# Eight raw weight places with in-place low parts, four places for high parts, and experts without a loop, in a two-block transformer on one core

## The reference

```python
def first_block(x, c, ...):
    cs = jax.nn.silu(c)
    for l in range(2):
        mod = cs @ w_ada[l] + b_ada[l]
        h = rmsnorm(x, g_pre[l]) * (1 + scale) + shift
        y = hybrid_mixer(h, w_in[l], w_out[l], ...)
        x = x + gate * rmsnorm(y, g_post[l])
    return x
```

## Time and profile before

| | |
|---|---|
| median of three runs | 1647.71 us |
| the profiled execution | 1648.49 us, its span 1646.7 us |
| mean granted TensorE clock | 0.94 of full speed |
| PE, DVE, ACT busy | 1420.0, 1216.3, 861.3 us |
| bytes of DMA | 403.08 MB, mean 245 GB/s |
| stages (us of the span) | pre to 47, lay0 to 255, lay1 to 465, na to 632, ffn to 884, mla to 1000, go to 1020, experts to 1553, `more` to 1619 |

### The profile page before, as it was taken

The page is one execution under the profiler, slowest core; times in us unless marked ns, Lnnn a source line. Parts: engine busy times, 40 slices in busy tenths (PEclk is TensorE's granted clock), DMA queues, the critical chain, the costliest instruction groups (busy, mean ns, idle before and its releaser), DMA issues.

```text
span 1646.7 us, 21231 instructions
## 1 busy us (share of the span) xinstructions
PE 1420.0 (86%) x7628; PEld 1189.7 (72%) x7628; DVE 1216.3 (74%) x1484; ACT 861.3 (52%) x1210; POOL 65.5 (4%) x82
## 2 busy tenths in 40 slices
PE   2798996989869986899985896999999999999992
PEld 1687776877658865898974785877777777777772
DVE  8676657766566646788866535889889888899885
ACT  0443544435443543344323544577677777777772
POOL 0000000000010000000001004000000000000001
PEclk9989998999988997999997996999999999999996
DMA  9763524735246632677773214799999999999782
GB/s 400 296 258 110 198 103 162 283 118 193 102 155 254 238 120 97 258 309 282 267 270 122 103 52 145 272 342 364 353 343 366 341 351 366 336 368 353 289 366 89
DMA packets 61538, 403.08 MB, mean 245 GB/s; under 512 B 6535, under 2 KB 9735, under 8 KB 15117
## 3 DMA queue, kind: packets, MB, share of 16 engines
q1 hardware_dynamic: 52416, 379.45, 60.7%
q10 hardware_dynamic: 7020, 15.17, 2.6%
q0 software_dynamic: 2016, 7.34, 1.2%
HBM read 393.01 MB, written 8.91 MB: 244 GB/s over the span
## 4 chain that ended last, share of the span: by engine, by line
PE 49%; DVE 31%; ACT 9%; issue 7%; DMA 2%; POOL 1%; ACTq 0%; DVEq 0%; SPq 0%; POOLq 0%
DVE w_lo L2175 18%; PE PS L826 13%; PE PS L828 12%; PE PS L827 12%; ACT w_hi L1601 4%; DVE acc L2192 3%; ACT xg L1695 2%; PE PS L978 1%; PE PS L998 1%; DMA raw<-in_ws 1%; DVE a_lo L2335 1%; PE PS L896 1%; DVE hb L2346 1%; DVE hb L2344 1%; DVE h_lo L2301 1%
## 5 line engine op out<-in xcount | busy, mean ns | idle before, releaser
L2175 DVE TENSOR_TENSOR w_lo<-raw,w_hi 128x2048 fp32r<-128x2048 f32 x287 | 659.5, 2298 | 147.7 <-ACT w_hi L1601 124.8
L1601 ACT ACTIVATE w_hi<-raw 128x2048 fp32r<-128x2048 f32 x287 | 547.7, 1918 | 235.1 <-PE PS L828 222.9
L826 PE MATMUL PS<-w_hi,h_hi 128*128 128x512 f32 (+2 forms) x812 | 336.6, 415 | 24.7 <-DVE h_lo L2596 7.3
L827 PE MATMUL PS<-w_lo,h_hi 128*128 128x512 f32 (+2 forms) x812 | 319.4, 393 | 0.0
L828 PE MATMUL PS<-w_hi,h_lo 128*128 128x512 f32 (+2 forms) x812 | 319.2, 393 | 0.0
L826 PE MATMUL PS<-h_hi,w_hi 128*128 128x256 f32 x776 | 235.4, 303 | 24.1 <-DVE h_lo L2220 11.2
L828 PE MATMUL PS<-h_hi,w_lo 128*128 128x256 f32 x776 | 227.1, 293 | 0.0
L827 PE MATMUL PS<-h_lo,w_hi 128*128 128x256 f32 x776 | 227.1, 293 | 0.0
L826 PEld LDWEIGHTS PS<-w_hi,h_hi 128*128 128x128 f32 x812 | 156.3, 192 | 72.0 <-DVE w_lo L2175 15.1
L2192 DVE SCALAR_TENSOR_TENSOR acc<-raw,cs,acc 128x512 f32<-128x512 f32 x252 | 189.5, 752 | 8.9
L828 PEld LDWEIGHTS PS<-w_hi,h_lo 128*128 128x128 f32 x812 | 156.1, 192 | 32.7
(11 more groups left out here) (310 smaller groups left out, 1405.8 us busy)
## 6 DMA issues: line engine op xcount, KB each, us to landing
raw<-in_ws SPq DMA_DIRECT2D x359, 1024.0 KB, 5.7
y_rows<-ysb ACTq DMA_DIRECT2D x10, 512.0 KB, 7.0
rp<-in_rp ACTq DMA_DIRECT2D x8, 384.0 KB, 4.7
ckb<-in_ck ACTq DMA_DIRECT2D x2, 1024.0 KB, 4.8
y_rows<-ones ACTq DMA_DIRECT2D x3, 512.0 KB, 9.2
x<-in_x SPq DMA_DIRECT2D x1, 1024.0 KB, 11.3
gpost<-in_gpost ACTq DMA_DIRECT2D x2, 512.0 KB, 5.3
x_rows<-xn_f ACTq DMA_DIRECT2D x2, 512.0 KB, 3.8
```

What stands on the lines that cost most here:

```text
L826: t.matmul(out, lhs[0], rhs[0], start=start, stop=False, skip_group_check=True)
L827: t.matmul(out, lhs[0], rhs[1], start=False, stop=False, skip_group_check=True)
L1601: a.activation(wh[:, SPL_AT[e.phase][i], :], raw[:, r, :], ACT.Copy).then_inc(*e.inc("hi"))
L2175: v.tensor_tensor(wl[:, s, :], raw[:, r, :], wh[:, s, :].bitcast(F32), ALU.subtract).then_inc(*e.inc("raw_used"))
```

## The change

1. RAW = 8 and SPL = 4. The low part is written over the raw step: `w_lo` is a second name for the memory of `raw`, so that there are 8 + 4 = 12 places of the same size. A place of a "w" step is now free when PE has done the block (`split_used`); that of an "ada" step still at `raw_used`. `ring_plan` gets, for each step, the semaphore that releases it.
2. The experts are moe0 to moe7, all written out on PE, ACT, DVE and SP. `more` is still a loop. `expert()` itself is not edited on any engine; its calls move with SPL.
3. The list of steps of lay has its last four "ada" halves after w12 to w15, where they were after w11 to w14; that of na has halves after w2 to w5 and w7 to w14, where it had them after w2 to w13.
4. Calls of `hi_to` and `split_to` in lay, na, mla move by one block, and by ticks in mla. In ffn, DVE's `split_to(n + 2 + SPL)` becomes `split_to(n + 1 + SPL)`, the same block as before, and ACT's `hi_to(n + 2 + SPL)` is one block further.

The core of the diff:

```diff
-RAW = 6
-SPL = 3
+RAW = 8
+SPL = 4
...
 def layer_steps():
-    halves = dict(zip((2, 3, 4, 5, 7, 8, 9, 10, 11, 12, 13, 14), ...))
+    halves = dict(zip((2, 3, 4, 5, 7, 8, 9, 10, 12, 13, 14, 15), ...))
...
 def na_steps():
-    halves = dict(zip(range(2, 14), ...))
+    halves = dict(zip((2, 3, 4, 5, 7, 8, 9, 10, 11, 12, 13, 14), ...))
...
+def raw_released(p, i):
+    if STEPS[p][i][0] == "w":
+        return "split_used", STEPS[p][i][1]
+    return "raw_used", i
+RAW_AT, RAW_NEED = ring_plan(RAW, {p: len(STEPS[p]) for p in PHASES}, raw_released)
+SPL_AT, SPL_NEED = ring_plan(SPL, SPLITS, lambda p, i: ("split_used", i))
...
-        wl = sb("w_lo", [P, SPL, STEP], F32R)
+        wl = nc.alloc_sbuf_tensor_at("w_lo", [P, RAW, STEP], F32R, offset=at[0] - 4 * RAW * STEP - 4 * SPL * STEP)
```

SP, `stream`:

```diff
-                        sp.wait_ge(*e.at("raw_used", RAW_NEED[phase][i]))
+                        sp.wait_ge(*e.at(*RAW_NEED[phase][i]))
```

DVE, `raw_to`:

```diff
-                        v.tensor_tensor(wl[:, s, :], raw[:, r, :], wh[:, s, :].bitcast(F32),
+                        v.tensor_tensor(wl[:, r, :], raw[:, r, :], wh[:, s, :].bitcast(F32),
```

PE (ACT, DVE and SP alike):

```diff
-                with pe.Fori(0, LOOPS) as rep:
-                    for p in TWO:
-                        e.enter(p, rep)
-                        expert()
-                e.enter("moeZ")
-                expert()
+                for p in EXPERTS[1:]:
+                    e.enter(p)
+                    expert()
```

ACT, lay:

```diff
-                hi_to(5)
+                hi_to(6)
                 slot(0)
-                hi_to(7)
+                hi_to(8)
                 slot(1)
                 ada_out(0, 1)
-                hi_to(8)
+                hi_to(9)
                 slot(2)
...
-                hi_to(9)
+                hi_to(10)
                 ada_out(1, 1)
```

In na, ACT's hi_to 5, 7, 9 become 6, 8, 10; in mla, its 5, 7, 8, 9 become 6, 8, 9 and none. DVE, ffn:

```diff
-                    split_to(n + 2 + SPL)
+                    split_to(n + 1 + SPL)
```

DVE, lay:

```diff
-                split_to(5)
+                split_to(6)
...
-                split_to(9)
+                split_to(10)
                 dve.wait_ge(*e.at("g_tanh", 1))
...
                 logits(0)
```

DVE, na, in the ticks:

```diff
-                    split_to(min(na_steps_before(i) + SPL, 15) if i < 14 else 16)
+                    split_to(min(na_steps_before(i) + SPL, 16))
```

More of the change, by code:

```diff
@@ L31 @@
 T_CMP = 15
-PHASES = ["pre", "lay0", "lay1", "na", "ffn", "mla", "rt", "go", "moe0", "moeA", "moeB", "moeZ", "more", "end"]
+EXPERTS = [f"moe{i}" for i in range(NEXP)]
+PHASES = ["pre", "lay0", "lay1", "na", "ffn", "mla", "rt", "go"] + EXPERTS + ["more", "end"]
 MORE = 2 * S // (P + 1)
 ROUNDS = NEXP + MORE
[L41 to L45, removed]
+REPS = {"more": MORE}
+KIND = {"lay0": "lay", "lay1": "lay", **{p: "moe" for p in EXPERTS}}
 LAY_FEAT = (0, 1, 4, 5)
@@ L136 @@
 }
-STEPS.update({p: [("w", i) for i in range(3 * MOE_SLOTS)] for p in ("moe0", "moeA", "moeB", "moeZ", "more")})
+STEPS.update({p: [("w", i) for i in range(3 * MOE_SLOTS)] for p in EXPERTS + ["more"]})
 STEPS = {p: STEPS.get(p, []) for p in PHASES}
@@ L173, in ring_plan @@
         pad = -n % size if reps > 1 else 0
[L174 to L178, removed]
-        for _ in range(reps):
[L180 to L187, removed]
+        place[p], need[p] = [(start + i) % size for i in range(n)], [None] * n
@@ L197 @@
 COUNTS = {
     "act": {"ffn": 22},
[L199 to L202, removed]
+    "act_hi": {"ffn": 22, "moe": 7, "more": 7},
+    "act_lo": {"moe": 7, "more": 7},
+    "act_tok": {"moe": 7, "more": 7},
+    "act_turned": {"moe": 7, "more": 7},
@@ L238 @@
     "downs_done": {"end": 1},
-    "dve": {"pre": 38, "lay": 82, "na": 47, "ffn": 105, "mla": 31, "rt": 10, "go": 23, "moe0": 11, "moeA": 7, "moeB": 7, "moeZ": 7, "more": 7},
+    "dve": {"pre": 38, "lay": 82, "na": 47, "ffn": 105, "mla": 31, "rt": 10, "go": 23, "moe0": 11, "moe1": 7, "moe2": 7, "moe3": 7, "moe4": 7, "moe5": 7, "moe6": 7, "moe7": 7, "more": 7},
     "dve_end": {"end": 21},
@@ L249 @@
     "hb_act": {"lay": 4, "na": 4, "ffn": 4, "mla": 4},
-    "hi": {"lay": 20, "na": 16, "ffn": 33, "mla": 9, "moe0": 21, "moeA": 21, "moeB": 21, "moeZ": 21, "more": 21},
+    "hi": {"lay": 20, "na": 16, "ffn": 33, "mla": 9, "moe": 21, "more": 21},
     "k_sum": {"mla": 2},
@@ L288 @@
     "rwb": {"mla": 1},
-    "saved": {"rt": 2, "moe0": 1, "moeA": 1, "moeB": 1, "moeZ": 1, "more": 1},
+    "saved": {"rt": 2, "moe": 1, "more": 1},
     "saved_last": {"end": 1},
@@ L318 @@
     "y_row3": {"end": 1},
-    "y_sb": {"moe0": 1, "moeA": 1, "moeB": 1, "moeZ": 1, "more": 1},
+    "y_sb": {"moe": 1, "more": 1},
     "y_sb_last": {"end": 1},
@@ L678, in _ @@
             first = None
-            for p in ("pre", "lay0", "lay1", "na", "ffn", "mla", "moe0", "moeA", "moeZ"):
+            for p in PHASES[:PHASES.index("more")]:
                 if p == "lay0":
```

123 lines of the change are left out of this document (52 added, 71 removed), and 8 rows, old and new, of the table COUNTS.

## The result

The changed kernel takes 1659.24 us (median of four runs, 1658.29 to 1662.81) against 1647.70 for the kernel before: ratio 1.007, 95% interval 1.0053 to 1.0087. The forecast was 1659, slower by over 0.3% with a chance of 0.60. The total came out to a quarter of a microsecond. The sum that led to it did not: it had +4.4 us ahead of the experts and +7.3 in them, and the trace has +10.5 and −0.6. An error of 6 us too little met one of 8 too much.

The account below looks back on a forecast made before the run. The prediction took the kernel as PE's work with waits for DVE between. Terms for lay0, lay1, na and the experts, 3.5 + 4.4 − 3.5 + 7.3 = +11.7 on 1648.5, less 0.8, gave 1659 us, range 1634 to 1670.

Parts of the forecast that it names:

- Written out: Six looped experts, unrolled: period 64.1 us, as in the already unrolled moeZ, instead of 65.5, 1.4 us saved each.
- DVE's order in the experts: Experts: `a_lo`(0) ends one `w_lo` later, 19.7 us after `ysb` starts; turn_act(1) gap 2.6 us, period 65.0.
- the wait before turn_act(6): Experts: PE's wait there grows by some 0.7 us, as `a_lo`(5) too stands behind one more `w_lo`.
- The clock: Experts: PE's clock falls to half after the 2.6 us gap in most experts, some 1.7 us each, period 66.7.
- the sum for the experts was −4 us: All experts and `more`, without falls of the clock: −2 − 3.0 + 0.9 + 0, −4 us; with them +7.3.
- `more`: The looped overfull expert: same order of work, less what ACT's waits for `raw` give back, +1.5 us.
- lay0, lay1: Two layer stages: more DVE work ahead of logits(0), partly hidden behind cmp1, adds +3.5 and +4.4 us.
- the −1.1 at the end of each layer: End of lay0 and lay1: one `w_lo` (2.3 us) less before the last `h_lo`, taken for half.
- the `w_lo` and `ada` ahead of logits(0): lay0, lay1: another half `ada` (3.11) and lo9 (2.3) before logits(0), +5.4 us.
- the late loads: lay and na: raw places held until PE is done make hi7 to hi9 up to 2 us later, beside DVE's 5.4.
- na: Stage na: the gap at w7 goes as `ada` of w6 comes later; −3.5 us (−5.7 to −1.2).
- Rival 1: Experts: the gap comes but the clock holds; +0.4, about 1648 us (1641 to 1655), chance 0.17.

Follow-up runs that it names:

- expert_order: The changed kernel with DVE's two splits of an expert's slot one block earlier, split_to(n + SPL) and split_to(n + 1 + SPL): 1632.34 us, ratio 0.9909.
- wider-gap kernel: The changed kernel with DVE's two splits of an expert's slot one block later, split_to(n + 2 + SPL) and split_to(n + 3 + SPL): 1717.88 us, ratio 1.0417.
- lay_lo9: The changed kernel with split_to(9) in place of split_to(10) ahead of logits(0) in lay, as before: 1663.62 us, ratio 1.0095.
- act_calls: The changed kernel with ACT's hi_to calls ahead of the first slots of lay and na put back as before: 1659.75 us, ratio 1.0097.

## Why the prediction was right, and where not

**Written out: right.** 1.4 us a period was read from moeZ, and the kernel with this alone has it.

**DVE's order in the experts: right, in mechanism and size.** `a_lo`(0) at T+19.8 for T+19.7, a gap of 2.52 for 2.6, no gap at blocks 14 and 20, a period of 65.1 for 65.0. One term was half its size: the wait before turn_act(6) is 1.4 us where moeZ shows 0.2, and a growth of 0.7 was forecast. (Its working does not come out either: four blocks and a turn of 0.25 in 1494.54 to 1506.22, less the wait, give 2.80 us a block and not 2.73, and with 2.80 there would have been no growth.) The expert_order kernel shows that the gap at turn_act(1) is the order and nothing else.

**The clock: wrong, and the largest error.** "I take it for most experts" failed: of seven gaps of 2.52 us one was followed by a fall (66.7 instead of 65.1, so the fall's price of 1.7 was right, 1.6 measured). I had read two rows as if the length of a gap decided. What sets these two apart from the six gaps that kept the clock is not shown: ahead of the one at 214.65 PE had been as busy, at full clock, as in an expert (4.10 of the 4.10 us from 208.0 to 212.1). The Trainium skill, "TensorE: Matmul & The Clock Gate" (its table of advice), which I had weighed and set aside, would have kept the clock through such a gap, and in six of seven the trace agrees; the seventh, and the falls of the wider-gap kernel, don't follow from it. Without the falls the sum for the experts was −4 us; measured were −0.6, with one fall (1.6) and the seam to `more` (3.6) in it.

**`more`: a term that was missing.** I costed its order and its loads and took its start for the same. The ring of places was never followed over the seam; it costs 3 to 4 us (2.8 between the medians of the two kernels, 3.8 in PE's idle time, 3.6 in the length of moe7). `more` itself was put at +1.5 and measured 0.

**lay0, lay1: the wrong step set the time.** lay1's +4.4 agrees by chance. It is not even the sum of its own terms: 5.4 − 2 − 1.1 and 5.4 − 1 − 1.1 are +2.3 and +3.3, not +3.5 and +4.4, so the −1.1 at the end of each layer was named and not added; it was there, −1.0 and −0.9 in the trace. With it the forecast would have been 1657. The forecast saw both mechanisms, priced the `w_lo` and `ada` ahead of logits(0) at 5.4, and put the late loads at "up to 2 us later than now, which lies beside DVE's 5.4 us above". It was the other way round: the loads, with ACT asked one block further ahead, moved cmp1 by 7.5 us, and logits(0) hid beside that. That is the step that failed: I counted how late the load is, and not that ACT now asks for that block ahead of the slot's copies, so that the wait is paid on the path to cmp1. Neither part does this alone: late release with the old calls moves cmp1 by 0 and 2.7 us, and the old calls in the changed kernel bring it from 7.5 to 1.0 us (2.7 and 0.3 in the two other kernels with them). But the two losses lie side by side, so neither is worth its own size: with cmp1 back, the forecast's wait for logits(0) comes out, and lay0 adds 2.7 to 5.8 us there instead of 4.9 to 6.3 (three and four traces).

**na: right in its mechanism, at a quarter of its size.** The gap went and the clock held (−7.3), but the ticks gave back 4.7 and the slots lost 1.7. The measured −0.8 lies just outside the stated bounds (−5.7 to −1.2). The slots' part is the step that failed in lay once more: with ACT's old calls they gain 0.8 or 0.9 and na adds −3.4 or −3.5, in three traces.

**The total** was right because 6 us too little ahead of the experts (of which up to 4 may be this one trace's) met 8 us too much in them. That is luck. Rival 1 (the gap comes, the clock holds) was nearer to what happened than the forecast; it would have said 1648, for want of lay's loads and of `more`.

## What to carry to other kernels

A deeper ring was a gain here only when the order of the work was kept: a call whose depth is written in terms of the ring's size moves ahead of work that another engine waits for when the ring grows (here undoing that in two lines turned +0.7% into −0.9%). An engine told to work further ahead must also find its data loaded, or it stands still with everything behind it on the path (here, PE's cmp1 7.5 us late). And follow a new ring size over every seam between stages: 21 blocks went evenly into three places and not into four.

## What the runs showed of the hardware

The granted clock does not answer to the length of a gap alone. The same gap of 2.52 us, with PE full before and after, was followed by a fall to 1.2 GHz in one of seven experts of one execution; with a second gap of 2.1 us 8 us ahead of it, in all seven. A gap of 1.62 us in a stage of small matmuls had been enough. A fall in an expert costs 1.6 us.

Which of several equal gaps is hit was the same in each trace that has them: the changed kernel, the lay_lo9 kernel and the act_calls kernel have the same seven gaps, and in all three the clock fell behind that of moe5 alone (at 1383.27, 1385.16 and 1376.93 us), though these executions are up to 8 us apart there. Why that one, and whether it is another in an execution without a trace, no run shows.

The sum of an engine's waits for loads is no price: ACT waited 97.6 us for them in ffn and the stage took 0.5 us longer, while of 15.0 us of them in lay0 some stood ahead of copies that PE needs, and cmp1 was 7.5 us late.
